# Experts' first tile: two low halves of weights made by GpSimd instead of VectorE, and two other steps moved on VectorE

## The reference

```python
x = x + g1 * y                                   # residual after the mixers
h = rmsnorm(x, norm_ffn_l) * (1.0 + sc2) + sh2
# hier_moe(h): top-1 group of four, then the top 2 of its four experts
glog = x @ w_rg;  gsel = argmax(glog)
elog_g = (x @ w_re)[group gsel]
top_p, top_i = top_k(softmax(elog_g), 2);  gate = gw * top_p / sum(top_p)
y = sum over experts of (silu(x @ w_g) * (x @ w_u) * gate) @ w_d
```

## Time and profile before

| | us |
|---|---|
| median of three timed runs | 1659.59 |
| profiled execution | 1658.35 |
| its span in the trace | 1656.8 |
| TensorE busy (share of the span) | 1624.4 (98%) |
| VectorE busy | 1004.9 (61%) |
| ScalarE busy | 864.5 (52%) |
| GpSimd busy | 643.0 (39%) |

### The profile page before, as it was taken

One profiled execution on the slowest core, in us unless ns is written; L12 is line 12 of the kernel. 1 busy time (PEld: TensorE's weight loads), 2 busy tenths in 40 slices (PEclk: granted clock), 3 DMA queues, 4 the chain that ended last, 5 costly groups with the idle time before them and its releaser, 6 DMA issues.

```text
span 1656.8 us, 26411 instructions
## 1 busy us (share of the span) xinstructions
PE 1624.4 (98%) x9831; PEld 1309.5 (79%) x9831; DVE 1004.9 (61%) x1664; ACT 864.5 (52%) x1458; POOL 643.0 (39%) x408
## 2 busy tenths in 40 slices
PE   7999999999999999999999999999999999999998
PEld 6788887777888887777768878777778888777776
DVE  4137477563451179999861484775634513999997
ACT  3444344444443347888744334454545334588884
POOL 1654453434467721000134555533345866110102
PEclk9999999999999999999999999999999999999999
DMA  9623344253556569999965334334354455899994
GB/s 370 233 94 101 115 141 142 93 185 140 200 200 244 208 235 402 390 378 377 327 243 189 102 106 145 113 130 147 133 186 160 171 180 216 317 397 380 403 373 160
DMA packets 127710, 365.62 MB, mean 221 GB/s; under 512 B 12012, under 2 KB 42348, under 8 KB 127600
## 3 DMA queue, kind: packets, MB, share of 16 engines
q1 hardware_dynamic: 93472, 318.23, 52.6%
q10 hardware_dynamic: 27504, 21.74, 4.2%
q0 software_dynamic: 6624, 24.18, 3.9%
HBM read 341.71 MB, written 22.39 MB: 220 GB/s over the span
## 4 chain that ended last, share of the span: by engine, by line
PE 82%; DVE 8%; issue 3%; ACT 2%; POOL 2%; DMA 1%; SPq 1%; POOLq 0%; ACTq 0%; DVEq 0%
PE G L1460 20%; PE G L1462 18%; PE G L1461 18%; PE S L1460 3%; PE S L1462 3%; PE S L1461 3%; PE T L1849 2%; DVE pA L2064 2%; PE O L1880 2%; PE S L1835 2%; PE O L1572 2%; DVE wlo L2064 1%; DVE pB L2064 1%; PE T L1751 1%; ACT whi L1050 1%
## 5 line engine op out<-in xcount | busy, mean ns | idle before, releaser
L896 POOL TENSOR_TENSOR wlo<-raw,whi 128x1024 fp32r<-128x1024 f32 x198 | 488.2, 2471 | 544.9 <-ACT whi L1039 530.1
L1460 PE MATMUL G<-whi,hhi 128*128 128x512 f32 (+1 forms) x1440 | 578.6, 402 | 10.3 <-DVE wlo L2064 5.6
L1462 PE MATMUL G<-whi,hlo 128*128 128x512 f32 (+1 forms) x1440 | 557.9, 387 | 0.0
L1461 PE MATMUL G<-wlo,hhi 128*128 128x512 f32 (+1 forms) x1440 | 557.4, 387 | 0.0
L1460 PEld LDWEIGHTS G<-whi,hhi 128*128 128x128 f32 x1440 | 270.6, 188 | 87.4 <-DVE wlo L2064 15.6
L1462 PEld LDWEIGHTS G<-whi,hlo 128*128 128x128 f32 x1440 | 270.5, 188 | 58.0
L1461 PEld LDWEIGHTS G<-wlo,hhi 128*128 128x128 f32 x1440 | 271.2, 188 | 46.8
L1039 ACT ACTIVATE whi<-raw 128x1024 fp32r<-128x1024 f32 x204 | 214.7, 1055 | 101.0 <-PE G L1462 76.5
L2064 DVE TENSOR_TENSOR wlo<-raw,whi 128x1024 fp32r<-128x1024 f32 x150 | 181.8, 1225 | 17.3 <-ACT whi L1050 7.8
L1050 ACT ACTIVATE whi<-raw 128x1024 fp32r<-128x1024 f32 x144 | 152.4, 1060 | 28.6 <-PE G L1462 16.2
L2064 DVE TENSOR_TENSOR wlo<-pA,whi 128x1024 fp32r<-128x1024 f32 x72 | 88.0, 1224 | 29.3 <-ACT whi L1050 25.0
(11 more groups left out here) (420 smaller groups left out, 2242.8 us busy)
## 6 DMA issues: line engine op xcount, KB each, us to landing
raw<-in_units SPq DMA_DIRECT2D x418, 512.0 KB, 5.2
pA<-in_units SPq DMA_DIRECT2D x75, 512.0 KB, 6.7
pB<-in_units SPq DMA_DIRECT2D x72, 512.0 KB, 6.5
h_sorted<-sig POOLq DMA_DIRECT2D x12, 514.0 KB, 7.2
hs<-h_sorted POOLq DMA_DIRECT2D x10, 514.0 KB, 7.4
y_sorted<-yo POOLq DMA_DIRECT2D x10, 512.0 KB, 7.0
bias<-in_nat_bias ACTq DMA_DIRECT2D x16, 256.0 KB, 3.4
pB<-rows_scratch ACTq DMA_DIRECT2D x8, 512.0 KB, 7.5
```

The costliest lines, as they stand in the source:

```text
L896: lo_done.of(nc.gpsimd.tensor_tensor(wlo[:, k, :], raw[:, POS_OF[g] % RAW, :], whi[:, k, :].bitcast(F32), ALU.subtract))
L1460: nc.tensor.matmul(dst, st_hi, mv_hi, start=start, stop=False)
L1461: nc.tensor.matmul(dst, st_hi, mv_lo, start=False, stop=False)
L1462: return nc.tensor.matmul(dst, st_lo, mv_hi, start=False, stop=stop)
```

## The change

GpSimd gets a function `early_low(n)`, which waits for the high half of unit n and for the low half of the unit before, and subtracts. In the step `("norm", 1)` it calls it for unit 1 ahead of the three root-mean-square steps and for unit 2 behind them. VectorE's `route` no longer makes these two. Its `rows_low(1)` and `unit_low(3)` (`CONV` is 3) move from behind the first maximum to behind the second, with a wait for GpSimd's unit 2 ahead of `unit_low(3)`; `unit_low(4)`, which stood behind the second maximum, now follows directly.

```diff
--- before.py
+++ after.py
@@ -595,7 +595,7 @@
         def bias_index(b):
             return b if b < 8 else (9 if b < 12 else 11)
 
-        def route(dve, need, own, tt, whole_row, rows_low, next_mods, unit_low):
+        def route(dve, need, own, tt, whole_row, rows_low, next_mods, unit_low, low_by_pool):
 
             V = nc.vector
             need(router_dve, ROUTER_BIAS)
@@ -656,21 +656,20 @@
             own(tt(cum, cum, gsel, ALU.mult))
             own(V.tensor_reduce(slot, cum, AX, ALU.add))
             slot_dve.of(V.tensor_scalar(slot_at[:, :].unsqueeze(2), slot, -1.0, None, ALU.add))
-            unit_low(1)
             rows_low(0)
-            unit_low(2)
 
             prod = rw[:, :, 32:48].rearrange("p t (g e) -> p t g e", g=4)
             own(tt(prod, el.rearrange("p t (g e) -> p t g e", g=4), gsel.unsqueeze(3).to_broadcast([P, TILES, 4, 4]), ALU.mult))
             own(V.tensor_reduce(rw[:, :, 28:32], prod.rearrange("p t g e -> p t e g"), AX, ALU.add))
             eg = rw[:, :, 28:32]
             first_max(eg, m1, sel1)
-            rows_low(1)
-            unit_low(CONV)
             own(V.tensor_scalar(rw[:, :, 48:52], sel1, NEG, None, ALU.mult))
             own(tt(rw[:, :, 48:52], rw[:, :, 48:52], eg, ALU.add))
             first_max(rw[:, :, 48:52], m2, sel2)
             rt_dve.of(tt(rw[:, :, 12:13], m2, m1, ALU.subtract))
+            rows_low(1)
+            dve.wait_ge(*low_by_pool)
+            unit_low(CONV)
             unit_low(CONV + 1)
             need(rt_act, 0)
 
@@ -896,6 +895,13 @@
                     lo_done.of(nc.gpsimd.tensor_tensor(wlo[:, k, :], raw[:, POS_OF[g] % RAW, :], whi[:, k, :].bitcast(F32),
                                                        ALU.subtract))
 
+                def early_low(n):
+
+                    pool.wait_ge(hi_done.handle, hi_done.value(l, NG + n))
+                    pool.wait_ge(*e_lo.in_tile(l, 0, UT, n - 1))
+                    e_lo.of(nc.gpsimd.tensor_tensor(wlo[:, n % CONV, :], expert_raw(n), whi[:, n % CONV, :].bitcast(F32),
+                                                    ALU.subtract))
+
                 def rstd(dst, src, n, width, signal):
                     if n == D:
                         own(nc.gpsimd.tensor_tensor(dst, src, cval[:, 1, 0:width], ALU.add))
@@ -910,9 +916,13 @@
                         if first:
                             pool.wait_ge(start_dve, 6)
                             first = False
+                        if s[1]:
+                            early_low(1)
                         for t in range(TILES):
                             pool.wait_ge(*sq_act.at(l, TILES * s[1] + t))
                             rstd_pool.of(rstd(st[:, t:t + 1], st[:, t:t + 1], D, 1, None))
+                        if s[1]:
+                            early_low(2)
                     elif s[0] in ("gemm", "rest"):
                         g = s[1]
                         if s[0] == "gemm" and g + 2 == CONV:
@@ -2473,7 +2483,7 @@
                                                          ALU.mult, ALU.subtract))
                     elif s == ("route",):
                         finish_route = route(dve, need, own, tt, whole_row, lambda hf: rows_low(hf, 0), next_mods,
-                                       lambda n: unit_low(0, n))
+                                       lambda n: unit_low(0, n), e_lo.in_tile(l, 0, UT, CONV - 1))
                     elif s == ("experts",):
                         def one_tile(i, last, first=False):
                             def hidden(e):
```

## The result

| | median, us | runs | lowest to highest | profiled execution | ratio, 95% interval |
|---|---|---|---|---|---|
| before | 1659.53 | 18 | 1658.1 to 1661.1 | 1658.35 | |
| changed | 1664.17 | 18 | 1660.0 to 1666.98 | 1663.65 | 1.0026 [1.0020, 1.0033] |

The changed kernel is 4.64 us slower; the forecast was 3.7 us slower. It also scatters over 7 us where the kernel before scatters over 3. A second measurement, beside other kernels, gave 3.81 us (1662.99 against 1659.18).

A forecast was written before the change was run, and what follows sets the result against it. TensorE, 82% of the chain of waits, was taken as the bound. A + B − C = 1.55 + 1.5 − 1.2 = +1.85 us per layer, +3.7 in all: median 1663.3 us, range 1658.4 to 1665.2 leaving out 2 in 10.

The forecast's parts named there:

- A: Before the router's logits: GpSimd's first subtraction, unit 1's, holds VectorE's residual addition; the logits' scaling starts late, 1.55 us per layer.
- both paths named: Logits' scaling near 599.4 either way: late product frees the logits' bank late, or the last root ends late at 599.3.
- B: In the group choice: GpSimd's second subtraction, unit 2's, holds VectorE's comparison, ending 601.85 instead of 600.3; 1.5 us per layer.
- C: Expert units: VectorE, rid of two low halves and reordered, delivers units 4 and 5 sooner; 1.2 us saved per layer.
- the 1.07 at unit 4: TensorE's wait of 1.07 us for unit 4's low half, forecast to go because VectorE makes that half sooner.
- The wait at unit 5: TensorE finishes unit 4 and the gate matmuls some 0.3 us before unit 5's low half: a short wait left.
- The sentence that C stays: Tile 1's gathered rows start from the gates, which come 1.25 us sooner, so C stays; DMA could take up to 0.6.
- rival 3: Scalings held too (+0.55), or C partly lost to tile 1's rows (up to 0.6); about 1665 us; chance 15%.
- both collisions: GpSimd's two subtractions holding VectorE's residual addition (A, 1.55 us) and its comparison in the group choice (B, 1.5 us).
- Rival 1: No collision: GpSimd's halves run beside VectorE, only C is left, −2.4 us, 1657.2; chance 8%.

The follow-up runs named there:

- e2_first: Kernel before with the changed VectorE order; GpSimd makes only unit 1's low half, ahead of the root-mean-square steps, VectorE unit 2's; 1659.57 us, ratio 1.0006.
- e3_second: Kernel before with the changed VectorE order; GpSimd makes only unit 1's low half, behind the last root, VectorE unit 2's; 1661.04 us, ratio 1.0016.
- e12_both8: Changed kernel plus 8 matmuls of a constant in each TensorE wait, for the group choice and at the layer border; 1659.79 us, ratio 1.0004.
- e8_again: Changed kernel as it is, measured once more beside other kernels; 1662.99 us, ratio 1.0022.
- e9_busy8: Changed kernel plus 8 matmuls of a constant in TensorE's wait for the group choice; 1660.86 us, ratio 1.0008.
- e5: Changed kernel plus 16 matmuls of a constant in TensorE's wait for the group choice; 1663.62 us, ratio 1.0026.
- e4: Kernel before, VectorE alone reordered: low halves of units 1 and 2 ahead of the rows' first half, second maximum behind their second; 1657.50 us, ratio 0.9994.
- e6: Changed kernel with each of GpSimd's two subtractions replaced by three zero fills of the same buffer; 1656.64 us, ratio 0.9981.

## Why the prediction was right

**A**, forecast 1.55 per layer: the scaling starts at 598.62 instead of 597.83 − 0.72, so 1.51. By itself, in e2_first, it makes the layers 1.65 and 1.55 longer. It came by both paths named: the product frees the bank late, and the last root is late too (0.50 <-POOL st).

**B**, forecast 1.5: TensorE's group choice at 601.54 instead of 599.43 − 0.72 is 2.83 late, so 1.32 beside A. By itself, in e3_second, it makes the group choice 1.13 and 1.19 late, and the layer without a fall 1.27 longer. Beside A it is 0.2 less because GpSimd's second subtraction ended sooner than I had put it: at 600.85 + 0.72 = 601.57 on the clock of before, not 601.8. It followed its root without a gap and took 2.35, not 2.4.

**C**, forecast 1.2 saved: the 1.07 at unit 4 is gone, and the stretch from router to second tile, where neither a fall nor a late row of tile 1 disturbs it (e12_both8), is 1.57 longer (88.40 against 86.83), which leaves 1.26 of the 2.83. In layer 1 the group choice is 2.83 late as well and the stretch 1.40 longer (88.42 against 87.02), so C is 1.4. The wait at unit 5, put at 0.3, is 0.16 as before (e8_again, e9_busy8 and e12_both8, layer 0). The sentence that C stays because the gathered rows come sooner too did not hold always: of ten layers measured under the changed order and GpSimd's halves (changed, e5, e8, e9, e12), three wait 0.77 to 1.03 us for tile 1's rows, and under the two kernels with the earliest routers (e4, e6) all four layers do. That is the price of up to 0.6 that rival 3 named, a little larger: layer 0 of the changed kernel's profile, with a wait of 0.79, is 0.99 longer than that of e12_both8.

So the sum of the layers is 1.57 + 1.40 = 2.97 where 3.7 was forecast: both collisions, and C, are there by the mechanism named, and B is the term that came out smaller. Three things stand beside this sum. The falls of the clock behind the lengthened wait, which the forecast has nowhere, cost some 2.0 to 2.8 us in the median by the filled runs. Tile 1's late rows cost up to 1 us in the layers where they come late. The collision at 946 us gives about 1.3 back if it is as regular as the profiles suggest, one profile of the kernel before with it and two of the changed kernel (the first and e8_again) without it. These terms offset each other in part. Without the falls the sum is 2.97 − 1.3 = 1.7, and e9_busy8, which has none behind the group choice, measured 1.81. That the forecast lies within 0.9 us of the first median, and within 0.2 of the second, is in that part luck; the mechanism of A, B and C is not.

On the falls: in the profiles here, waits of 0.73 us or less at the group choice were followed by a fall in none of 16 layers, waits of 1.87 to 2.05 in 3 of 6, and filled ones in none of 6; the wait of 2.14 at the border in 6 of 11, filled in none of 3. The Trainium skill (TensorE: Matmul & The Clock Gate, section "What's actually happening") states that the gate looks at TensorE's activity in a window that runs free of the program, so that where a stretch meets it differs between executions. By that the same idle stretch costs in one execution and not in the next, and the spread widens with the median; the trace agrees in so far as waits of 2.05 us were followed by a fall in two of the changed kernel's four layers. That the window decides which ones is not shown.

Rival 1 (no collision) would have been right for a GpSimd that only writes, as e6_write shows with 2.54 under. Rival 3 was the nearest miss: its price for tile 1's rows is real, but the scalings were not held.

## What to carry to other kernels

An operation that is moved to an idle GpSimd, and reads SBUF there, can still cost time on VectorE: an operation of VectorE with both inputs in SBUF that starts inside it waits until it is done (1.69 and 1.32 us here, of 2.4). Place it by VectorE's rows, not by GpSimd's. A wait on TensorE that grows from under one to two microseconds may cost nearly its length once more, in some executions (1.4 to 1.6 us a fall here, once 3.3); read the granted clock behind it, and the spread of the runs. And where two kernels differ in a stretch that no edit touches, look there for a race between two engines that went the other way.

## What the runs showed of the hardware that was not expected

- The granted clock fell to 0.50 behind idle stretches as short as 1.87 us, and stayed there for 3.4 to 7 us of full work; one fall cost 1.4 to 1.6 us, the longest some 3.3 (92.74 − 88.42, less the 1.03 for tile 1's rows).
- In a collision of VectorE and GpSimd it matters which starts first, even by little: 0.11 us behind GpSimd's start cost VectorE 2.17 us (2.86 against 0.69), 0.25 ahead of it cost GpSimd 0.26 (2.67 against 2.41).
- A scaling with one input in PSUM, one in SBUF and a column of factors was not held by GpSimd's reading (0.24 and 0.38, as before).
